# Copies that move a product to the other 64 partitions, made by VectorE instead of ScalarE in two of the six passes

## The chip, the cores and the metric

The kernel runs on one core of one Trainium2 chip. The metric is the time of the whole program on the device in microseconds (us), median over its runs; lower is better. TensorE multiplies matrices from SBUF into PSUM, which here is eight banks of 128 partitions by 512 float32 values. VectorE, ScalarE and GpSimd work on tiles beside it.

## The reference, cut to what matters

The program computes two model blocks of two layers each, for 256 positions of width 1024, in float32. The part that the change touches is in layer 0 of the first block: a recurrence over 256 context and 256 latent positions, run forwards and backwards.

```python
def _rwkv7_scan(S0, r, w, k, v, kk, a):
    def step(S, inp):
        r_t, w_t, k_t, v_t, kk_t, a_t = inp
        sa = jnp.einsum('bhvk,bhk->bhv', S, kk_t)
        S = (S * w_t[:, :, None, :] - sa[..., None] * (kk_t * a_t)[:, :, None, :]
             + v_t[..., None] * k_t[:, :, None, :])
        return S, jnp.einsum('bhvk,bhk->bhv', S, r_t)
...
    yf_c, Sf_c = _rwkv7_scan(S0, r_c, wf_c, k_c, v_c, kk_c, a_c)
    yf_l, _ = _rwkv7_scan(Sf_c, r_l, wf_l, k_l, v_l, kk_l, a_l)
```

There are 8 heads of 64 channels. Everything else of the two blocks (attention, other recurrences, projections, gated layers) is left as it is.

## The kernel before, in words

The recurrence is computed in 8 chunks of 64 positions. `rwkv_chunks_stage(net, d)` does it once for each direction: d = 0 forwards, and later in the program d = 1 backwards. Two heads share a tile, one in the lower and one in the upper 64 partitions (`o` is the half, `half(o)` its slice), and two chunks make a pair, `cp`; the four pairs are handled in the order x = 0 to 3, with PSUM banks 2x and 2x+1 for pair x. Within a chunk the positions depend on each other, so each head needs the inverse of a 64 by 64 triangular matrix. The kernel builds it in `N_LEVELS` = 5 levels, each of which doubles the size of the blocks inverted so far.

A stage is a block of its own with a barrier at its end; all its engines run their own instruction streams and wait for each other by semaphores. In the streams of one chunk stage stand:

- TensorE: `products` of the keys for each pair (L3172, L3182, L3183) and transposes (L3189); then `across` (L3199) for x = 0 to 3, the products with values, called level 0 below; then a hardware loop of five passes (L3215, `pe.Fori`), each with four `across` for the level and, behind them, four inverse products (L3231, L3232). The loop's register arithmetic sets the values waited for. Every `across` fills half a bank for chunk q = 0 and half a bank for q = 1; the inverse product needs both copied to SBUF, that of q = 1 with its halves of partitions exchanged.
- ScalarE: `copy_tokens` (L2848), the copies of the transposes, 32 in a stage; then per level (0 to 5) and pair one copy of 128 partitions for q = 0 (L3322) and two of 64 partitions that exchange the halves for q = 1 (L3324). The last of the three raises `y_copied`.
- VectorE: masks on the products (L3344, L3349); then per level and pair two subtractions that update the inverse (L3358), and in the first seven cases one multiplication by the decays (L3362). They raise `doubled`.
- GpSimd: masks for the next level (L3304, L3298), raising `level_ready`.

After the fifth level the chunks are gone through one by one (L3240 to L3287 on TensorE, L3367 to L3391 on VectorE). SyncE issues no transfers in this stage. The trace shows small transfers of 16 KB on queue 8, which the profile calls instruction.

## Time and profile before

| what | value |
|---|---|
| median of 3 runs | 2006.39 us (2005.78 to 2009.97) |
| the profiled execution, its own time | 2003.86 us |
| its span, first to last instruction | 2002.0 us |
| granted TensorE clock, mean over the span | 0.966 of full speed |
| TensorE busy with matmuls | 1849.9 us (92%) |
| VectorE busy | 1252.0 us (63%) |
| ScalarE busy | 858.9 us (43%) |

A row of the profile that groups instructions names line, engine, operation and tiles, the count, busy time and mean of one in ns. A row of the timeline gives start and length in us, and in brackets how long the engine stood idle before and what released it. "issue" there means that the profile shows nothing that the engine waited for. Times in the trace count from the span's start. The clock of TensorE is given as a share of its full 2.4 GHz, so 0.50 is 1.2 GHz.

### The profile page before, as it was taken

Reading aid. Unit: us, or ns where it says so; the run is one execution under the profiler, and the core shown is the slowest. Engines: PE = TensorE matmul, PEld = TensorE weight load, DVE = VectorE, ACT = ScalarE, POOL = GpSimd, SP = SyncE. Lnnn points to the kernel's source line nnn. Section 1 sums busy time; section 2 is a strip of 40 time slices with the busy share of each in tenths; the row PEclk is TensorE's granted clock in tenths of the full one; section 3 lists DMA queues with packets and bytes.
Section 4 is the critical chain, followed back from the end, with each engine's and each line's share of the span. In section 5 each row is a group of like instructions: output and inputs, shape, how many; then the busy total and the mean of one; then the engine's idle time right before and its main releaser. Section 6 shows DMA issues by size and latency. Waiting matters only on the chain. (4 is left out here: it accounts for less than half of the span.)

```text
span 2002.0 us, 42924 instructions
## 1 busy us (share of the span) xinstructions
PE 1849.9 (92%) x18352; PEld 1619.1 (81%) x18352; DVE 1252.0 (63%) x2170; ACT 858.9 (43%) x1588; POOL 289.3 (14%) x341
## 2 busy tenths in 40 slices
PE   7999887878899999999999699999789999889997
PEld 5787546857588888888878699999589999679997
DVE  4574786676657523543766778745668756677753
ACT  4321566446334211221537445534654345564432
POOL 0201203314040000013002111012030012021001
PEclk8999888979999999999999899999899999999998
DMA  9752750020523232322420356554135465225543
GB/s 323 208 175 84 255 188 3 2 65 2 163 76 100 85 105 84 105 85 85 147 64 1 100 178 188 188 185 155 43 127 190 148 190 190 85 85 190 190 153 100
DMA packets 248982, 254.68 MB, mean 127 GB/s; under 512 B 6914, under 2 KB 247186, under 8 KB 248690
## 3 DMA queue, kind: packets, MB, share of 16 engines
q1 hardware_dynamic: 239214, 242.85, 37.9%
q10 hardware_dynamic: 8740, 8.51, 1.3%
q8 instruction: 121, 1.98, 0.4%
q0 software_dynamic: 864, 0.98, 0.3%
q14 instruction: 43, 0.35, 0.1%
HBM read 251.28 MB, written 1.05 MB: 126 GB/s over the span
## 5 line engine op out<-in xcount | busy, mean ns | idle before, releaser
L529 DVE TENSOR_TENSOR RING_rounded<-RING,SC_rounded 128x1024 fp32r<-128x1024 f32 (+2 forms) x390 | 462.1, 1227 | 229.9 <-ACT SC_rounded L522 229.4
L549 PE MATMUL bank<-OT_rounded,SC_rounded 128*128 128x256 f32 (+1 forms) x1808 | 575.7, 318 | 14.5 <-DVE HT_rounded L1115 6.8
L550 PE MATMUL bank<-HT_rounded,SC_rounded 128*128 128x256 f32 (+1 forms) x1808 | 570.8, 316 | 0.0
L551 PE MATMUL bank<-OT_rounded,RING_rounded 128*128 128x256 f32 (+1 forms) x1808 | 569.2, 315 | 0.0
L522 ACT ACTIVATE SC_rounded<-RING 128x1024 fp32r<-128x1024 f32 (+2 forms) x390 | 372.6, 1006 | 331.2 <-DMA RING<-in_l_mlp_w 184.1
L549 PEld LDWEIGHTS bank<-OT_rounded,SC_rounded 128*128 128x128 f32 x1808 | 343.5, 190 | 43.8 <-DVE HT_rounded L1115 7.6
L551 PEld LDWEIGHTS bank<-OT_rounded,RING_rounded 128*128 128x128 f32 x1808 | 342.8, 190 | 25.5
L550 PEld LDWEIGHTS bank<-HT_rounded,SC_rounded 128*128 128x128 f32 x1808 | 342.9, 190 | 21.7
L549 PE MATMUL bank<-PT_rounded,SC_rounded 128*128 128x256 f32 (+1 forms) x896 | 277.6, 310 | 5.1 <-DVE RING_rounded L529 5.1
L550 PE MATMUL bank<-PT_rounded,SC_rounded 128*128 128x256 f32 (+1 forms) x896 | 276.7, 309 | 0.0
L551 PE MATMUL bank<-PT_rounded,RING_rounded 128*128 128x256 f32 (+1 forms) x896 | 276.0, 308 | 0.0
L549 PEld LDWEIGHTS bank<-PT_rounded,SC_rounded 128*128 128x128 f32 x896 | 168.5, 188 | 17.0 <-DVE RING_rounded L529 6.3
L551 PEld LDWEIGHTS bank<-PT_rounded,RING_rounded 128*128 128x128 f32 x896 | 168.3, 188 | 10.7
L550 PEld LDWEIGHTS bank<-PT_rounded,SC_rounded 128*128 128x128 f32 x896 | 168.4, 188 | 9.5
L550 PE MATMUL bank<-OT_rounded,SC_rounded 128*128 128x256 f32 (+1 forms) x336 | 101.2, 301 | 0.0
L549 PE MATMUL bank<-HT_rounded,SC_rounded 128*128 128x256 f32 (+1 forms) x272 | 84.3, 310 | 13.4 <-DVE OT_rounded L1468 5.5
L796 DVE SCALAR_TENSOR_TENSOR XT<-bank,MOD,XT 128x256 f32<-128x256 f32 x48 | 21.3, 479 | 112.6 <-PE bank L551 112.6
L551 PE MATMUL bank<-HT_rounded,RING_rounded 128*128 128x256 f32 (+1 forms) x272 | 83.1, 306 | 0.0
L3358 DVE TENSOR_TENSOR SC<-SC,bank 128x512 f32<-128x512 f32 (+1 forms) x80 | 50.9, 681 | 35.6 <-PE bank L3232 35.1
L776 ACT ACTIVATE PT<-bank 128x512 f32<-128x512 f32 x32 | 18.9, 598 | 123.6 <-PE bank L551 123.6
L838 DVE TENSOR_TENSOR PT<-PT 128x512 f32<-128x512 f32 x32 | 22.1, 690 | 74.7 <-ACT PT L776 74.7
L550 PEld LDWEIGHTS bank<-OT_rounded,SC_rounded 128*128 128x128 f32 x336 | 64.8, 193 | 2.2
(570 smaller groups left out, 2805.9 us busy)
## 6 DMA issues: line engine op xcount, KB each, us to landing
RING<-in_l_mlp_w SPq DMA_DIRECT2D x64, 1024.0 KB, 5.3
RING<-in_w_ffn_in SPq DMA_DIRECT2D x44, 1024.0 KB, 5.1
RING<-in_l_mod_w SPq DMA_DIRECT2D x32, 1024.0 KB, 5.5
RING<-in_l_w_in SPq DMA_DIRECT2D x25, 1024.0 KB, 6.3
RING<-in_w_ffn_out SPq DMA_DIRECT2D x16, 768.0 KB, 4.8
RING<-in_w_in SPq DMA_DIRECT2D x10, 1024.0 KB, 5.2
RING<-in_w_ffn_out SPq DMA_DIRECT2D x16, 640.0 KB, 4.3
PT<-in_l_mod_w SPq DMA_DIRECT2D x8, 1024.0 KB, 10.4
```

The costliest lines, as they stand in the source:

```text
L522: act.activation(net.high4(s, m)[:, 0:self.w.kts[s], :], net.ring_half(net.RING, s, m, self.w.kts[s]), ACT.Copy).then_inc(self.high_ready, 1)
L529: net.nc.vector.tensor_tensor(low, whole, net.high4(s, m)[:, 0:self.w.kts[s], :].bitcast(F32), ALU.subtract).then_inc(self.split_ready, 1)
L549: net.nc.tensor.matmul(bank[:, tokens], high, x_high, start=start, stop=False)
L550: net.nc.tensor.matmul(bank[:, tokens], high, x_low, start=False, stop=False)
L551: return net.nc.tensor.matmul(bank[:, tokens], low, x_high, start=False, stop=stop)
L776: act.activation(hidden.whole[:, 2 * q + m, :], part.bank(q, m)[:, :], ACT.Relu).then_inc(part.taken, 1)
L796: return nc.vector.scalar_tensor_tensor(into, bank[:, tokens], net.MOD[:, gate + tile, j:j + 1], into, ALU.mult, ALU.add)
L838: link(nc.vector.tensor_tensor(whole, whole, whole, ALU.mult))
L3358: nc.vector.tensor_tensor(inv, inv, bank, ALU.subtract).then_inc(doubled, 1)
```

## The change

At level 0 and at level 1 the two copies that exchange the halves go from ScalarE to VectorE. ScalarE keeps the plain copy and raises `y_copied` after it. VectorE raises a new semaphore, `y_swapped`, for which TensorE waits too, once in every `across` and once in every inverse product of the loop. From level 2 on ScalarE makes all three copies as before.

```diff
             with pe.Fori(0, N_LEVELS):
                 for x, cp in enumerate(pairs):
                     pe.wait_ge(y_copied, y_done(0, x))
+                    pe.wait_ge(y_swapped, y_done(0, x))
                     pe.wait_ge(level_ready, level_at)
...
                 for x, cp in enumerate(pairs):
+                    pe.wait_ge(y_swapped, y_done(1, x))
                     pe.wait_ge(y_copied, y_at)
...
-                    act.activation(first, same, ACT.Copy)
-                    for h in range(2):
+                    step = act.activation(first, same, ACT.Copy)
+                    for h in range(2 if lv > 1 else 0):
                         step = act.activation(second[half(1 - h)], swapped[half(h)], ACT.Copy)
                     step.then_inc(y_copied, 1)
...
+            for lv in range(2):
+                for x, cp in enumerate(pairs):
+                    dve.wait_ge(y_ready, y_done(lv, x))
+                    swapped = net.ps[2 * x + 1][:, 0:256].rearrange("p (t m) -> p t m", t=4)
+                    second = mem.y[x][1] if lv else mem.gram[:, 2 * cp + 1, 1, :, 0, :]
+                    for h in range(2):
+                        step = nc.vector.tensor_copy(second[half(1 - h)], swapped[half(h)])
+                    step.then_inc(y_swapped, 1)
             for lv in LV:
```

On ScalarE, where level 0 and level 1 of the forward stage stand, the program before has these rows (RING is the tile of level 0, PT and SC those of `mem.y`):

```order
L2848 ACTIVATE HT<-bank 64x4x64 x4
L3322 ACTIVATE RING<-bank 128x4x64
L3324 ACTIVATE RING<-bank 64x4x64 x2
...
L3322 ACTIVATE PT<-bank 128x256
L3324 ACTIVATE PT<-bank 64x256 x2
...
L3322 ACTIVATE SC<-bank 128x256
L3324 ACTIVATE SC<-bank 64x256 x2
```

The changed program has these at the same place, with its own line numbers (L3324 is now the plain copy, L3326 the exchange):

```order
L2848 ACTIVATE HT<-bank 64x4x64 x4
L3324 ACTIVATE RING<-bank 128x4x64 x4
L3324 ACTIVATE PT<-bank 128x256 x2
L3324 ACTIVATE SC<-bank 128x256 x2
L3324 ACTIVATE PT<-bank 128x256
L3326 ACTIVATE PT<-bank 64x256 x2
```

The first eight plain copies now follow each other, and the exchanges begin at level 2. On VectorE the sixteen exchanges stand between the last mask and the first subtraction (L3368, which was L3358):

```order
L3351 TENSOR_TENSOR SC<-bank,CONST 128x256 x4
L3359 COPY RING<-bank 64x4x64 x8
L3359 COPY PT<-bank 64x256 x4
L3359 COPY SC<-bank 64x256 x4
L3368 TENSOR_TENSOR SC<-SC,bank 128x2x256 x2
L3372 TENSOR_TENSOR PT<-PT,SC 128x4x128
```

In the difference of TensorE's rows, with what each waits for, the first `across` of the loop reads so:

```order
-L3219 REGISTER_ALU [waits rwkv_chunks0_level_ready,rwkv_chunks0_y_copied]
-L3221 REGISTER_ALU [waits rwkv_chunks0_doubled]
+L3220 REGISTER_ALU [waits rwkv_chunks0_level_ready,rwkv_chunks0_y_swapped,rwkv_chunks0_y_copied]
+L3222 REGISTER_ALU [waits rwkv_chunks0_doubled]
 L3199 MATMUL bank<-SC 64x64 x16
```

No matmul moves; one wait is added ahead of each of the 8 groups of matmuls of a pass, 40 in a stage of five passes.

## Rows read from the trace of the kernel before

**Rows 1.** The page, parts 1 and 3; windows over both stages up to level 5
```profile
PE 1849.9 (92%) x18352; PEld 1619.1 (81%) x18352; DVE 1252.0 (63%) x2170; ACT 858.9 (43%) x1588; POOL 289.3 (14%) x341
...
q8 instruction: 121, 1.98, 0.4%
...
core 0: us, PE busy (x) PEld busy (x) DVE busy (x) ACT busy (x) POOL busy (x), PEclk, DMA share, GB/s
317.00:380.00 63.00, 52.37 (x2584) 49.05 (x2578) 43.50 (x77) 39.52 (x104) 33.27 (x44) 0.96 0.01 2
437.00:495.50 58.50, 52.14 (x2507) 48.40 (x2500) 40.30 (x73) 39.53 (x104) 33.66 (x44) 0.94 0.01 3
```

**Rows 2.** Timeline of ScalarE, forward stage, levels 0 and 1
```profile
333.51 1.55 ACT L2848 ACTIVATE HT<-bank 64x256 f32<-64x256 f32 x4
335.08 0.39 ACT L3322 ACTIVATE RING<-bank 128x256 f32<-128x256 f32 x1
335.48 0.77 ACT L3324 ACTIVATE RING<-bank 64x256 f32<-64x256 f32 x2
336.27 0.38 ACT L3322 ACTIVATE RING<-bank 128x256 f32<-128x256 f32 x1
...
343.81 0.77 ACT L3324 ACTIVATE SC<-bank 64x256 f32<-64x256 f32 x2
```

**Rows 3.** Timeline of VectorE, forward stage
```profile
331.97 1.40 DVE L3349 TENSOR_TENSOR SC<-bank,CONST 128x256 f32<-128x256 f32 x4
342.35 1.28 DVE L3358 TENSOR_TENSOR SC<-SC,bank 128x512 f32<-128x512 f32 x2 [8.98 <-PE bank L3232]
343.55 0.68 DVE L3362 TENSOR_TENSOR PT<-PT,SC 128x512 f32<-128x512 f32 x1
...
348.64 1.28 DVE L3358 TENSOR_TENSOR SC<-SC,bank 128x512 f32<-128x512 f32 x2
```

**Rows 4.** Timeline of TensorE, forward stage: level 0's last group and pass 1
```profile
335.20 0.69 PE L3199 MATMUL bank<-SC,RING 64*64 64x64 f32 x32 [0.99 <-ACT HT L2848]
336.47 0.69 PE L3199 MATMUL bank<-SC 64*64 64x64 f32 x32 [0.58 <-ACT RING L3324]
...
340.04 0.69 PE L3199 MATMUL bank<-SC 64*64 64x64 f32 x32 [0.50 <-ACT RING L3324]
341.13 0.24 PE L3231 MATMUL bank<-PT,SC 64*64 64x64 f32 x1 [0.40 <-ACT PT L3324]
...
344.54 0.27 PE L3231 MATMUL bank<-PT,SC 64*64 64x64 f32 x1 [1.16 <-issue]
...
348.23 0.27 PE L3231 MATMUL bank<-SC 64*64 64x64 f32 x1 [1.60 <-issue]
348.94 3.65 PE L3199 MATMUL bank<-SC 64*64 64x64 f32 x128 [0.36 <-issue]
```

**Rows 5.** Windows of the forward stage: instruction transfers and TensorE's stops
```profile
337.00:338.00 1.00, 0.51 (x33) 0.41 (x28) 0.00 (x0) 0.95 (x4) 0.73 (x2) 1.00 0.08 16
342.00:343.00 1.00, 0.97 (x66) 0.86 (x60) 0.65 (x2) 0.95 (x3) 0.00 (x0) 1.00 0.05 16
345.00:346.00 1.00, 1.00 (x83) 1.00 (x78) 1.00 (x2) 0.00 (x0) 0.00 (x0) 1.00 0.07 16
347.00:348.00 1.00, 0.00 (x0) 0.00 (x0) 1.00 (x3) 0.00 (x0) 0.00 (x0) 1.00 0.00 0
344.50:348.00 3.50, 2.09 (x127) 1.96 (x127) 3.06 (x6) 0.07 (x1) 0.00 (x0) 1.00 0.02 5
348.00:353.00 5.00, 4.41 (x179) 4.30 (x183) 2.50 (x5) 2.79 (x8) 4.08 (x7) 0.66 0.00 0
```

**Rows 6.** Timeline of TensorE, backward stage: level 0's end and pass 1
```profile
452.19 0.57 PE L3199 MATMUL bank<-SC,RING 64*64 64x64 f32 x21 [0.17 <-issue]
454.56 0.97 PE L3199 MATMUL bank<-SC 64*64 64x64 f32 x32 [0.58 <-ACT RING L3324]
455.75 3.51 PE L3199 MATMUL bank<-SC 64*64 64x64 f32 x96 [0.21 <-ACT RING L3324]
461.45 0.26 PE L3231 MATMUL bank<-PT,SC 64*64 64x64 f32 x1 [0.18 <-issue]
465.47 0.21 PE L3231 MATMUL bank<-SC 64*64 64x64 f32 x1 [1.86 <-issue]
466.86 0.35 PE L3199 MATMUL bank<-SC 64*64 64x64 f32 x9 [0.23 <-issue]
```

**Rows 7.** Durations by source line: VectorE's copy, ScalarE's exchange
```profile
L3377 DVE COPY SC<-bank x2: 409/409/409, 381.9 to 497.7; 128x256 f32<-128x256 f32 x2
L3324 ACT ACTIVATE SC<-bank x40: 376/380/382, 342.6 to 493.7; 64x256 f32<-64x256 f32 x40
L3358 DVE TENSOR_TENSOR SC<-SC,bank x80: 673/679/692, 342.4 to 497.1; 128x512 f32<-128x512 f32 x64, 64x512 f32<-64x512 f32 x16
```

**Rows 8.** Timelines of ScalarE and TensorE, a later pass
```profile
366.62 0.38 ACT L3322 ACTIVATE PT<-bank 128x256 f32<-128x256 f32 x1 [3.51 <-PE bank L3199]
...
370.58 0.77 ACT L3324 ACTIVATE SC<-bank 64x256 f32<-64x256 f32 x2
373.61 0.38 ACT L3322 ACTIVATE PT<-bank 128x256 f32<-128x256 f32 x1 [2.26 <-PE bank L3199]
...
372.86 2.44 PE L3199 MATMUL bank<-SC 64*64 64x64 f32 x128 [0.22 <-DVE SC L3358]
```

More of the change, by code:

```diff
@@ L3158, in rwkv_chunks_stage @@
         kv_ready, values_ready, values_copied = st.sem("kv_ready"), st.sem("values_ready"), st.sem("values_copied")
-        own, decayed = st.sem("dve_own"), st.sem("decayed")
+        own, decayed, y_swapped = st.sem("dve_own"), st.sem("decayed"), st.sem("y_swapped")
         carried = lambda j: (mem.far if j % 2 else mem.near)[:, :, chunks[j] // 2]
```

## The prediction

> **What bounds the kernel now.** I read the page first, then windows over the two chunk stages, then one engine's timeline after the other. The page's shares say little here: TensorE is busy 92% of the program [rows 1], but this change lives in levels 0 and 1 of two stages, 63.0 and 58.5 us long with all that leads up to them [rows 1], of 2002.0. The stages are closed by barriers and issue no transfers of weights, so what one of them gains should reach the end nearly whole.
>
> In the forward stage ScalarE ends the copies of the transposes at 335.06 and goes straight on with 8 groups of copies, 0.39 + 0.77 and a short gap, one group every 1.19 us, until 344.58 [rows 2]. VectorE ends its masks at 333.37 and then stands idle for 8.98 us [rows 3]. TensorE starts its last group of level 0 at 335.20 and then waits 0.58 to 0.40 us before each of five groups, released by ScalarE's exchange each time [rows 4]. Read that far, ScalarE is the bound and VectorE is free.
>
> The reader should read one row further. At 344.54 TensorE comes back from an idle 1.16 us, and at 348.23 from 1.60 us, both put down to "issue" [rows 4]. The second stands in the middle of the inverse product of pair 3, whose copy was done at 344.58: nothing that the change touches holds it. The page has a queue named instruction, with 121 transfers of 1.98 MB in all, 16 KB each [rows 1]. The windows show 16 KB moved in the microsecond from 342, and 16 KB in that from 345, and TensorE at rest from 347 to 348 [rows 5]. Between the two stops 127 matmul and 127 weight-load rows lie [rows 5], with the register instruction ahead of each product (one or two here) about 256 instructions: a block of code, which TensorE consumes and then stands still until the next has come. The backward stage repeats it, with stops that end at 452.19, 461.45 and 465.47 [rows 6]. From the second pass on the same code is run again and such stops don't recur.
>
> The crossings into a new block, counted back by 256 instructions, lie in the forward stage at about 335.9 (the loop's start), 340.5 (near the end of the fourth `across`), 344.54 and 348.23; in the backward one at 452.19, 457.1 (early in the third `across`), 461.45 and 465.47 [rows 4, 6]. So a block comes 3.7 to 4.4 us after the one before it was entered, and usually about 4.0. Only two crossings, 340.5 and 457.1, are late because of ScalarE: TensorE arrived there after the code.
>
> **The change, part by part.** *Removed from ScalarE:* 2 exchanges by 4 pairs by 2 levels by 2 stages, 32 by 0.38 [rows 7] = 12.2 us. Level 0 gets a pace of 0.40 us a pair in place of 1.19.
>
> *Added on VectorE:* the same 32 copies. No row shows a PSUM copy of 64 partitions by 256; the nearest is one of 128 by 256 at 409 ns [rows 7]. The lower bound is nothing, the upper the 679 ns of an operation on 512 columns [rows 7]. I take 0.41, the same columns and source, so at most 0.82 a pair and 6.6 a stage. The cover is the idle 8.98 us. At 0.82 a pair level 0's exchanges start at 333.4 and the fourth, whose product ends near 335.9, is done by 336.8; TensorE can't enter the next block before 339.6, so even at 1.36 a pair (done at 338.8) it stays hidden. Without that cover the two of the last pair would cost 0.8 a level. Queued behind them is VectorE's first subtraction, which starts at 342.35 now [rows 3]; level 1's last exchange should end by about 341, so it is not late.
>
> The Trainium skill ("VectorE: DVE Perf Modes", the errata section's cycle table) prices a PSUM copy at 120 + columns cycles of 0.96 GHz on VectorE and 172 + columns of 1.2 GHz on ScalarE; I estimate from it 392 ns against 357, so it speaks against the move by 0.035 each, or 1.1 us if all 32 lay on the path. The rows here say 409 against 380, the same sign; as they lie in parallel with ScalarE and with the wait for code, neither puts anything into the sum.
>
> *Gain, forward stage.* Data no longer delays TensorE: its fourth `across` of the loop would reach the crossing at 335.9 + 4 by 0.59 (a group of 32 takes 0.69, overlapping the next by 0.1 [rows 4]) = 338.3. The code comes at 335.9 + 4.0 = 339.9 (339.6 with 3.7) instead of a crossing at 340.5. The next two follow by the same intervals: 343.7 and 347.5 instead of 344.54 and 348.23. I take 0.9 (0.6 by intervals of 4.0, 1.2 by 3.7).
>
> *Gain, backward stage.* 452.19 + 4.0 = 456.2, and TensorE's data is there by 455.3; then 460.2 and 464.2 instead of 465.47, a gain of 1.3. If the load isn't asked for earlier than now it is 0.7. I take 1.0.
>
> *Added on TensorE:* 40 waits a stage. I take each as one more instruction of the sequencer, which no row of the trace shows by itself. Where the loop turns, the idle is 0.36 and 0.23 us [rows 4, 6] for the branch, register work and three waits, so one is at most 0.12 and may be nothing where the sequencer runs ahead; I take 0.1. In pass 1 the wait for code hides all. In passes 2 to 5 ScalarE copies without a pause from 366.62 to 371.35 at 1.19 a pair [rows 8], slower than TensorE's inverse product (66 matmul rows in 0.97 us [rows 5], so 64 in 0.95), so the waits ahead of inverse products 2 to 4 lie under its copies. Exposed is the one ahead of the first `across` of a pass, which comes right behind the branch: 4 passes by 2 stages by 0.1 = 0.8 us.
>
> *Sum:* -0.9 - 1.0 + 0.8 = -1.1 us. The profiled execution took 2003.86 (span 2002.0), so it would take about 2002.8; the median of the runs shown lies 2.5 above the profiled one, and 2006.4 - 1.1 = 2005.3.
>
> **The rivals.**
>
> *Code is not the limit.* If the blocks came as early as TensorE wanted them, the forward loop would turn at 335.9 + 4 by 0.59 + 4 by 0.95 = 342.1 in place of 348.9. VectorE then limits: its first subtraction starts at 335.9 + 4 by 0.59 + 0.95 = 339.3, and at 1.28 + 0.68 less an overlap of 0.1 a pair its fourth ends at 339.3 + 3 by 1.86 + 1.28 = 346.2, now 349.92 [rows 3]. That is 3.7 us earlier, and the `across` behind it at full clock gives up to 1.2 more: some 4 to 5 us a stage, 9 together, less 0.8 for the waits: 1998. For it speaks ScalarE's release of five groups [rows 4]; against it two stops with nothing else to wait for and a 16 KB transfer ahead of each [rows 5]. By the Trainium skill ("Runtime: NRT & Kernel Launch", Instruction fetch mechanics) the sequencer fetches the next 16 KiB block, 256 instructions, while the present one runs, and crossing is mostly hidden: by that rule this rival would come true. The trace agrees on the size of a block and not on the hiding: 1.16, 1.60 and 1.86 us of stop. 8 in 100.
>
> *The gain is eaten.* The load is asked for no earlier, the stages gain 0.3 and 0.5, and the waits take 0.8 or a little more, as more of them show: 2006 to 2008. 16 in 100.
>
> *The waits decide, slower.* TensorE's own pace is the limit in passes 2 to 5 and all 80 waits show: 80 by 0.1 = 8, less 1.9, is +6, so 2012.5. It counts as slower from about 60 of 80 exposed. Against it is ScalarE's slower pace there [rows 8]. 5 in 100.
>
> *The clock moves.* After the two stops of the forward stage the granted clock is 0.66 from 348 to 353, that is partly 1.2 GHz, and four `across` take 3.65 us [rows 5, 4] where they take 2.44 at full clock [rows 8]: 1.2 us. In the backward stage level 1's three groups take 3.51 for 96 matmuls [rows 6]. Which stretch runs at the lower level may change, as TensorE rests earlier and longer before a load; one such stretch more or less is 1 to 2 us either way, and up to 4 if it hits both stages: 11 in 100, of which 4 end faster than 0.2%, 2 slower (the forecast already lies on the fast side) and 5 between.
>
> **How the numbers follow.** 0.2% of 2006.4 is 4.0 us, about what a measurement of this kernel can tell from none. The forecast as summed has the other 60 in 100. Faster by more than that: the first rival's 8, and 4 for clock and block boundaries falling well. Slower: the wait rival's 5, and 2 of the clock's. The rest, 81, is the same. The range leaves out the first and third rival at their full size, and takes in the bounds of the loads, the clock and the 2.5 us between executions: 2001.0 to 2008.5.
>
> **What the profile after would show.** Right: ScalarE's plain copies 0.40 apart at levels 0 and 1 and 64-partition COPY rows of about 0.41 on VectorE in its former idle time; TensorE's waits for ScalarE at 336.47 to 341.13 gone, and in their place longer "issue" stops, ending some 4 us apart, with the 16 KB transfers ahead of them; the loop's first turn only 0.5 to 1.3 us earlier after the last transposes than now; later passes at 7.0 us (373.61 - 366.62 [rows 8]) as before or 0.1 longer. Wrong: a first turn near 342 would make the first rival true; a pass of 7.4 or more the third; exchanges over 0.7 us, or a VectorE that ends them after 342.3, would break the cover. Since code shifts by 8 instructions in the loop, a stop can also fall just before the end of a product on which VectorE waits; the sum has nothing for that.

## The result, and the profile after

The changed kernel took 2008.43 us (median of 20 runs, 2002.98 to 2013.80), the kernel before 2005.40 in its 20 runs beside it (2002.29 to 2009.97). The ratio is 1.0016, 95% interval [1.0009, 1.0024]: slower by a little, within 0.2%. The forecast was right that the change is small, and had the sign wrong: 1.1 us faster was summed, 3.0 us slower was measured.

The page, and the two stages in windows, to be read against [rows 1]:

```profile
PE 1858.6 (93%) x18352; PEld 1625.7 (81%) x18352; DVE 1267.1 (63%) x2202; ACT 846.4 (42%) x1556; POOL 287.4 (14%) x341
...
q8 instruction: 121, 1.98, 0.4%
...
core 0: us, PE busy (x) PEld busy (x) DVE busy (x) ACT busy (x) POOL busy (x), PEclk, DMA share, GB/s
317.00:380.00 63.00, 54.10 (x2587) 50.63 (x2579) 50.97 (x93) 33.38 (x89) 33.45 (x44) 0.94 0.01 2
437.00:495.50 58.50, 50.48 (x2333) 47.11 (x2329) 45.62 (x85) 31.57 (x84) 33.30 (x44) 0.91 0.01 3
```

ScalarE gave 32 exchanges (858.9 to 846.4 us, x1588 to x1556), VectorE took them. Fewer matmuls lie in the backward window than before (2333, before 2507): the stage is late there. ScalarE and VectorE in the forward stage, against [rows 2, 3]:

```profile
335.10 1.26 ACT L3324 ACTIVATE RING<-bank 128x256 f32<-128x256 f32 x4
337.49 0.85 ACT L3324 ACTIVATE PT<-bank 128x256 f32<-128x256 f32 x2 [1.14 <-PE bank L3199]
...
333.41 3.52 DVE L3359 COPY RING<-bank 64x256 f32<-64x256 f32 x8
337.49 1.74 DVE L3359 COPY PT<-bank 64x256 f32<-64x256 f32 x4 [0.56 <-PE bank L3199]
...
341.21 0.86 DVE L3359 COPY SC<-bank 64x256 f32<-64x256 f32 x2 [1.09 <-PE bank L3199]
342.26 1.29 DVE L3368 TENSOR_TENSOR SC<-SC,bank 128x512 f32<-128x512 f32 x2 [0.18 <-PE bank L3234]
```

Eight exchanges take 3.52 us, 0.44 each (0.41 was taken), and they end before VectorE's first subtraction, which starts at 342.26 as it did (342.35). TensorE's first pass, against [rows 4] and, for the backward stage, [rows 6]:

```profile
335.22 0.69 PE L3199 MATMUL bank<-SC,RING 64*64 64x64 f32 x32 [0.99 <-ACT HT L2848]
336.74 2.13 PE L3199 MATMUL bank<-SC 64*64 64x64 f32 x122 [0.83 <-POOL SC L3300]
340.82 0.34 PE L3199 MATMUL bank<-SC 64*64 64x64 f32 x6 [1.95 <-issue]
...
344.72 0.37 PE L3233 MATMUL bank<-PT,SC 64*64 64x64 f32 x1 [1.03 <-issue]
348.72 0.35 PE L3234 MATMUL bank<-SC 64*64 64x64 f32 x1 [0.29 <-issue]
```

```profile
456.72 1.15 PE L3199 MATMUL bank<-SC 64*64 64x64 f32 x61 [1.21 <-issue]
460.71 0.21 PE L3234 MATMUL bank<-SC,PT 64*64 64x64 f32 x1 [1.90 <-issue]
464.89 0.26 PE L3233 MATMUL bank<-SC 64*64 64x64 f32 x1 [0.76 <-issue]
```

The waits for ScalarE at 336.47 to 341.13 are gone: 122 matmuls run through. In their place stand stops that end at 336.74, 340.82, 344.72 and 348.72, that is 4.1, 3.9 and 4.0 us apart, the last three for nothing that the profile shows. (The first row names GpSimd, but its product for this pair was done at 324.8.) A 16 KB transfer on the instruction queue starts ahead of each of the last three, at 338.14, 342.05 and 345.95. The intervals of about 4.0 us are as forecast; only the chain started 0.8 us late (336.74, where 335.9 was assumed), so all of it is later than the forecast 339.9, 343.7 and 347.5, and no earlier than before. Such a late start needs no change of the kernel: TensorE's sequencer rests 0.79 us ahead of the loop here, 0.09 in the profile of before, and 0.68 in a second profile of the same kernel before. The granted clock is 0.50 from 343 to 348, where before had full clock up to 348; the stops become shorter by it and end no later. In the backward stage the stops end at 456.72, 460.71 and 464.89, the last two 0.7 and 0.6 us earlier than before (forecast 460.2 and 464.2).

One later pass is seen best in ScalarE, whose first copy of a pass follows TensorE's first group at a fixed distance:

```profile
366.03 0.38 ACT L3324 ACTIVATE PT<-bank 128x256 f32<-128x256 f32 x1 [3.55 <-PE bank L3199]
373.17 0.38 ACT L3324 ACTIVATE PT<-bank 128x256 f32<-128x256 f32 x1 [2.40 <-PE bank L3199]
```

7.14 us, where [rows 8] have 6.99 (373.61 - 366.62).

**How the experiments are compared.** Every kernel was run some 12 times (the one with a filler 6), with 23 to 35 runs of the kernel before beside it; single runs of one kernel spread over 3 to 13 us. Much of that spread follows the mean granted clock of the run: over 383 runs (two with a clock of 0.918 and 0.919, one of before and one of the code shift, are left out, as the line doesn't fit them) a straight line with one constant for each kernel has a slope of -0.93 +- 0.04 us for 0.001 of clock, and leaves 1.5 us. So beside each ratio stands the kernel's constant minus that of before, "at the same clock", with its standard error; an unchanged copy shows what that is worth. For the changed kernel it is +1.3 +- 0.4 (against the runs of before in the other sets, as the clocks of the 20 beside it are not on record). What a change costs by lowering the clock itself is not in that column; the section behind the experiments comes to it.

### The profile page after: what moved, and what is told of

It is laid out like the page before. It is cut to its first block and busy times, and to the rows that moved or that the text cites. A ratio compares the mean times of both kernels' runs of the same rounds, so it can differ in the third digit from the quotient of the medians.

```text
span 2006.4 us, 42966 instructions
## 1 busy us (share of the span) xinstructions
PE 1858.6 (93%) x18352; PEld 1625.7 (81%) x18352; DVE 1267.1 (63%) x2202; ACT 846.4 (42%) x1556; POOL 287.4 (14%) x341
## 5 line engine op out<-in xcount | busy, mean ns | idle before, releaser
L550 PEld LDWEIGHTS bank<-HT_rounded,SC_rounded 128*128 128x128 f32 x1808 | 342.9, 190 | 21.8
L549 PEld LDWEIGHTS bank<-HT_rounded,SC_rounded 128*128 128x128 f32 x272 | 52.8, 194 | 16.7 <-DVE RING_rounded L529 9.9
```

Of the source, the lines that this page charges most:

```text
L549: net.nc.tensor.matmul(bank[:, tokens], high, x_high, start=start, stop=False)
L550: net.nc.tensor.matmul(bank[:, tokens], high, x_low, start=False, stop=False)
```

## The experiments

**The kernel before again**, not a character changed.

> The kernel before, run as if it were a new one: the floor of the comparison, and the granted clock beside the time of each of its runs. Two theories stand for the 3.2 us (0.16%) that the change costs. Clock theory: the change by itself costs nothing, but TensorE's rests lie earlier and longer, the granted clock falls to 1.2 GHz in stretches that are on the path, and the time of a run follows its mean granted clock; the kernel before then has a higher mean clock, by about 0.002 or more, than the changed one's runs (0.960 to 0.969, mean about 0.963), and the two lie on one line of time over clock. Wait theory: the 80 added waits on TensorE cost it directly; the clocks are then the same, and at the same clock the changed kernel is 3 us slower. Both expect 1.000 here, within 0.001.

2003.62 against 2006.15, ratio 0.9993 [0.9982, 1.0003], at the same clock +0.1 +- 0.5. Its mean clock was 0.0014 above that of the others: a difference of 1.2 us in the mean comes by chance, and the column at the same clock removes it.

**The waits alone.** TensorE's stream is that of the changed kernel, ScalarE makes all copies and raises the new semaphore after its plain copy.

```diff
-                    act.activation(first, same, ACT.Copy)
+                    step = act.activation(first, same, ACT.Copy)
+                    if lv < 2:
+                        step.then_inc(y_swapped, 1)
```

> The 40 added waits a stage alone: ScalarE makes all copies as in the kernel before, and raises y_swapped itself, earlier than y_copied, so that no wait holds anything longer. Wait theory: all or most of the loss, +2 to +3.5 us (1.0010 to 1.0017). Clock theory: only the wait at the loop's turn shows, +0.8 us (1.0004), and the granted clock is that of the kernel before. In the profile a later pass of the forward stage should take 7.0 us plus 0.1 by either.

2009.37, ratio 1.0016 [1.0004, 1.0028], at the same clock +1.5 +- 0.5: the waits without any copy moved cost as much as the whole change.

**The copies alone.** The exchanges move to VectorE, but ScalarE waits for them; TensorE's stream is that of before.

```diff
+                    if lv < 2:
+                        act.wait_ge(y_swapped, y_done(lv, x))
-                    act.activation(first, same, ACT.Copy)
-                    for h in range(2):
+                    step = act.activation(first, same, ACT.Copy)
+                    for h in range(2 if lv > 1 else 0):
```

> The whole move of copies to VectorE, with TensorE's stream left exactly as in the kernel before: no added wait there. ScalarE waits for y_swapped ahead of its plain copy at levels 0 and 1 and then raises y_copied for both. Wait theory (the added waits cost some 1.2 us directly and lower the granted clock by about 0.002, worth 2 us more): the loss is gone, ratio 0.999 to 1.0000, mean clock 0.965 or more, and later passes take 7.0 us. If the moved copies themselves lower the clock by making TensorE's rests in pass 1 longer: mean clock about 0.963 and ratio 1.001.

2004.70, ratio 0.9988 [0.9977, 1.0000], at the same clock -1.8 +- 0.5. What the move itself gives is near the summed -1.9; the step that failed lies in the waits.

**Data sooner.** The changed kernel with the copies of levels 0 and 1 cut short, and `mem.y` zeroed at the stage's start. The edit does less than its expectation says: its rows are 64x64 and 128x64, so 64 of 256 columns are copied and not 4, in 0.22 us in place of 0.42 on VectorE and 0.38 on ScalarE. It leaves out the other 192 columns.

> The changed kernel with the copies of levels 0 and 1 cut to one column of each head's 64 (the rest of those products is left out and stands as zeros written at the stage's start), so the data of pass 1 is there almost at once. If the blocks of code set the pace of pass 1, the loop of the forward stage turns where it does in the changed kernel (349.1, 14.0 us after the last group of level 0 at 335.2) or at most 0.5 us earlier, and the time stays within 2 us of the changed kernel's. If the copies set it, the loop turns near 342 to 343 and the time falls by 8 us or more (0.997 against the kernel before).

2007.98, ratio 1.0007 [0.9994, 1.0020], at the same clock +1.1 +- 0.5. Copies a quarter of the size gain nothing clear of the error over the changed kernel (+1.3), and the first pass still stops, until 338.85, 342.75 and 346.66, 3.9 us apart. The first rival ("Code is not the limit") is out.

**One wait for four.** The changed kernel with one wait for four pairs ahead of the loop, and one a pass ahead of the inverse products.

```diff
+            pe.wait_ge(y_swapped, 4)
             with pe.Fori(0, N_LEVELS):
...
-                    pe.wait_ge(y_swapped, y_done(0, x))
...
+                pe.wait_ge(y_swapped, 8)
...
-                    pe.wait_ge(y_swapped, y_done(1, x))
```

> The change with its copies on VectorE, but with one wait ahead of the loop and one a pass ahead of the inverse products in place of eight a pass. Wait theory: the loss goes away and the gain of 1 to 1.9 us that the summing gave is seen (0.9990 to 0.9996). Clock theory: still slower by 2 to 3 us (1.0010 to 1.0015), as the rests of pass 1 are as long as in the changed kernel, or longer since inverse product 0 waits for the exchange of pair 3.

2007.58, ratio 1.0004 [0.9992, 1.0017], at the same clock +1.3 +- 0.5. A later pass takes 7.00 to 7.03 again, and the time is not back: the number of waits isn't all of it. One wait for four also holds the first pass until the last pair's exchange is done, so this run doesn't isolate the number.

**A shift of the code, no wait.** The kernel before with two unused 64x64 matmuls a stage ahead of the loop, which put all that follows 8 instructions further.

```diff
+                if x == 0:
+                    for n in range(2):
+                        nc.tensor.matmul(net.ps[0][half(0), 256 + at(n).start:256 + at(n).stop], ident[half(0), half(0)],
+                                         ident[half(0), half(0)], start=True, stop=True)
```

> The kernel before with two matmuls of 64 by 64 more ahead of level 0 in each stage (8 instructions on TensorE, no further wait, the result unused), so that all code behind them lies 8 and then 16 instructions later, as the change does it. If the place of the code blocks makes the loss: 1.001 or more. If it doesn't: 1.0000, mean clock 0.965, with some 0.1 us for the matmuls.

2008.37, ratio 1.0014 [1.0001, 1.0028], but its clock was low: at the same clock +0.6 +- 0.5. The same two matmuls in the variant with the copies alone:

> The variant in which ScalarE waits for VectorE's copies (-1.8 us at the same clock), plus the two unused 64x64 matmuls a stage ahead of the products with values that shift all that follows by 8 instructions. Theory A: no wait added, so the gain stays but for the 0.1 us that the matmuls take: -1.5 +- 0.5 us at the same clock, ratio 0.9992. Rival (the place of the rows in the 16 KB blocks of code takes the first pass's gain away): 0 to +0.5 us at the same clock, ratio 1.0000 to 1.0005, and the first pass of a stage no shorter than before.

2006.56, ratio 1.0004 [0.9995, 1.0012], at the same clock +0.3 +- 0.5, 2.1 +- 0.6 above the variant without them. The rival written there fits: 8 more instructions in front can cost. Beside before they cost +0.6 +- 0.5, so their size is less sure, and that they act by their place in the blocks of code is not shown by these two runs.

**A filler.** The changed kernel with one unused 128x256 matmul a pass ahead of the fourth `across`.

> The changed kernel with one matmul of 128 by 256 more in each pass of the loop, ahead of the fourth group with values, into a free half of a bank (its result unused). It takes some 0.4 us of TensorE's time in each pass, under ScalarE's copies. If the loss comes by way of the granted clock because TensorE rests a little too much in the passes: the mean clock goes up to 0.965 or more and the time goes down by 1 us or more against the changed kernel (1.001 or less against the one before). If the waits cost directly alone: clock as in the changed kernel (0.963) and 1 to 3 us slower than it (1.002 to 1.003).

2013.09, ratio 1.0039 [1.0025, 1.0054], at the same clock +6.5 +- 0.6. Ten such matmuls cost 5 us over the changed kernel, and no clock is bought with them. TensorE's idle time there isn't free.

**The last pair.** The kernel before with the exchange of pair 3 on VectorE at all levels, ScalarE waiting for it.

> From the kernel before: VectorE makes the two exchanges of the last pair (x = 3) at every level, 0 to 5, and ScalarE waits for them ahead of its plain copy of that pair; TensorE's stream is unchanged. Where ScalarE sets the pace of a pass (7.0 us: four groups of 1.19 and the turn), its last group shrinks by 0.77 us, VectorE being idle 1.84 us just then. If passes 4 and 5 and partly 2 and 3 are bound by ScalarE: passes 4 and 5 take about 6.4 us and the time falls by 2 to 4 us (0.998 to 0.999). If TensorE's own time in a pass (about 6.3 us with the turn) or VectorE binds right behind: under 1 us.

2004.25, ratio 0.9993 [0.9982, 1.0004], at the same clock -1.1 +- 0.5; a pass at full clock takes 6.73. Together with the copies alone (levels 0 and 1 of all pairs, levels 2 to 4 of pair 3):

> VectorE makes the exchange of all four pairs at levels 0 and 1 and that of pair 3 at levels 2 to 4; ScalarE waits for it ahead of its plain copy, and TensorE's instructions are those of the kernel before. The two parts alone gave -1.7 and -1.0 us at the same clock (the second with level 5, where it lengthened the chunk phase by 0.6 a stage). Theory that what the copies give is real and additive: -2.5 to -3 us, ratio 0.9985 to 0.9988, passes at full clock 6.73 to 6.75 us from pass 2 on and the fill pass shorter by 1 us a stage. Rival (code blocks limit the first pass, so only one of the two shows there; and a shorter pass lowers or shifts the clock): -1.5 to -2, ratio 0.9991.

2005.17, ratio 0.9996 [0.9984, 1.0008], at the same clock -0.4 +- 0.5: the two gains don't add up. The theory missed; the passes did come to 6.73 and 6.78, and the third pass took 8.46 in the backward stage (7.71 in the copies alone). In that kernel VectorE's last multiplication by the decays takes 1.12 us, where the copies alone have 0.68; the section on VectorE and GpSimd below shows what that comes from.

**Which waits.** The waits alone, cut to those ahead of `across`, and to those ahead of the inverse products.

> ScalarE keeps all copies; of the 80 added TensorE waits only the 40 ahead of the products with values stay (20 a stage). Every one of them but those of level 0 stands ahead of an `across` group. Theory A (each added wait costs its time wherever it stands, the number decides): half of what all 80 cost against the kernel before at the same granted clock (1.5 us), so +0.8, and half of the fall of the mean clock (0.0019), so -0.001; in all about +1.7 us, ratio 1.0008. Theory B (only waits that stand in front of a group that starts when a product is just done cost, which my prediction had: the first group of `across` of a pass): +0.8 of time here and nothing from the waits ahead of the inverses; a pass at full clock 7.10 us. Theory C (the rows' place in the code blocks decides, not the waits): a change of 1 to 3 us in the length of passes 2 and 3 against the kernel before, in either direction, with the time in no order with the number of waits.

> The other half: only the 40 added TensorE waits ahead of the inverse products (20 a stage). Theory A: +0.8 us at the same clock, clock lower by 0.001, in all +1.7 us, ratio 1.0008, as for the waits ahead of `across`. Theory B: nothing, time as before within 0.5 us at the same clock, a pass at full clock 7.00 us. Theory C: 1 to 3 us in passes 2 and 3, in either direction.

2006.13, 1.0003 [0.9992, 1.0013], at the same clock -0.3 +- 0.5; and 2008.69, 1.0013 [1.0003, 1.0024], +1.7 +- 0.5. ScalarE's first copies of two passes, first kernel, then second:

```profile
366.54 0.38 ACT L3323 ACTIVATE PT<-bank 128x256 f32<-128x256 f32 x1 [3.52 <-PE bank L3199]
373.53 0.38 ACT L3323 ACTIVATE PT<-bank 128x256 f32<-128x256 f32 x1 [2.26 <-PE bank L3199]
```

```profile
367.58 0.38 ACT L3323 ACTIVATE PT<-bank 128x256 f32<-128x256 f32 x1 [3.55 <-PE bank L3199]
374.72 0.39 ACT L3323 ACTIVATE PT<-bank 128x256 f32<-128x256 f32 x1 [2.40 <-PE bank L3199]
```

6.99 and 7.14 us. It is the other way round than forecast: the waits ahead of the inverse products are paid, those ahead of `across` are not. Theories A and B both missed.

**Twice the waits.** A second satisfied wait behind each of the 80.

> All 80 added TensorE waits and, behind each, one more on a second semaphore that has long been raised: 160 added waits. Theory A: twice what 80 cost: +3.0 us at the same clock, clock lower by 0.004, in all +6.6 us, ratio 1.0033; a pass at full clock 7.25 us. Theory B: +0.8 becomes +1.6, clock no lower than with 80, in all about +4, 1.002. Theory C: no order with the number; between 0.999 and 1.002, and a pass at full clock still 7.13.

2008.79, 1.0012 [1.0003, 1.0021], at the same clock +2.8 +- 0.5, pass 7.20. The lower clock that was expected did not come.

**The order of the waits.** In the changed kernel and in the waits alone, the order ahead of `across` turned round; and in the waits ahead of `across` alone, the added wait moved to the last place.

```diff
+                    pe.wait_ge(y_swapped, y_done(0, x))
                     pe.wait_ge(y_copied, y_done(0, x))
-                    pe.wait_ge(y_swapped, y_done(0, x))
                     pe.wait_ge(level_ready, level_at)
```

The expectations of the first two have this wrong: ahead of the inverse products the changed kernel and the waits alone already wrote the added wait in front of the one for ScalarE's copies, as the diff of the change shows, and the edit left it there. So their theory A was not put to the test at the place where the cost lies.

> The changed kernel, with one thing turned round: each of the 80 added TensorE waits stands ahead of the wait for ScalarE's copies and no longer behind it. Number of instructions, copies and semaphores are as in the changed kernel. Theory A (a wait costs only where it stands behind the wait that ends last: ahead of the inverse products that is the wait for ScalarE's copies, so that the added one is worked off after the data is there, 0.12 us in a pass): all of the cost of the waits goes, a pass at full clock takes 7.00 us and not 7.13, pair 3's inverse products start 5.61 us into a pass and not 5.76, and the time is that of the variant in which ScalarE waits: -1.8 us against the kernel before at the same clock, ratio 0.9991. Theory B (each wait costs by being there, or the shift of the code that the added instructions make costs): as the changed kernel, +1.3 us at the same clock, ratio 1.0010 to 1.0016, pass 7.13. A mix (pass 7.00 but time still above -1): the order of the waits is the smaller part, and something else in the first pass is the rest.

> ScalarE keeps all copies; the 80 added waits are there, each ahead of the wait for ScalarE's copies. Theory A: the added waits cost nothing: 0 +- 0.5 us against the kernel before at the same clock (behind it: +1.5), ratio 1.0000, pass at full clock 7.00 us. Theory B: +1.5 us, ratio 1.0010 to 1.0016.

> ScalarE keeps all copies; only the 40 added waits ahead of the products with values, but each as the last of the waits there, behind the one for the inverse (`doubled`), where the variant before had it second of four and cost nothing. Theory A (behind the wait that ends last, it is paid): up to 0.1 us at the first group of each pass, and at pair 3's group, 0.1 to 0.2 us a pass, pass at full clock 7.10 to 7.20, +1 to +2 us at the same clock. Theory B (its place among the waits does not matter, waits ahead of `across` are cheap): 0 +- 0.5 us, pass 7.00.

2007.48, 1.0009 [0.9998, 1.0019], +1.3 +- 0.5; 2009.39, 1.0015 [1.0005, 1.0024], +2.5 +- 0.5; 2009.50, 1.0015 [1.0005, 1.0025], +1.7 +- 0.5. The first two kept their passes of 7.10 to 7.18. The third made passes of 7.10 to 7.14 out of 6.99 with the same number of waits. TensorE's own records of its sequencer, beside the matmuls, say why: they show which instruction carries which wait. (A semaphore has a number there; that of y_copied is known from before, whose inverse products wait for nothing else.) Microseconds from the first weight load of a pass at full clock, around pair 3's inverse products:

```
                semaphore instruction   register addition    first weight load
before          none                    y_copied   5.552     5.612
waits_values    none                    y_copied   5.553     5.613
changed         y_copied   5.555        y_swapped  5.696     5.756
wait_ahead      y_copied   5.544        y_swapped  5.684     5.745
```

A register addition carries one wait. A second one makes a semaphore instruction of its own in front of it. Which wait goes where follows the source in every kernel here: the one written first goes to the addition, the rest to the semaphore instruction (ahead of `across` it is y_copied that the addition carries in the changed kernel, and y_swapped with the order turned round). Ahead of the inverse products the added wait was written first. So the addition got y_swapped, long raised, and the semaphore instruction got y_copied, the wait that ends last; the addition is then worked off only behind it. That costs 0.11 to 0.14 us. With y_copied written first, the semaphore instruction would hold the satisfied wait and could be worked off ahead of time. No run tried that.

The Trainium skill ("Perfetto Trace Analysis", Identifying Dependency Chains) says that EventSemaphore instructions may be inserted ahead of an instruction that waits for several engines; the trace agrees and adds the price. Ahead of `across` before already had such an instruction with one wait in it, and the added one went into it free. Written last, behind the first addition, it made another one there (at 6.977, for 0.1 us at a pass's start).

**A register addition to carry it.** The changed kernel with an addition on an unread register behind the wait.

> The changed kernel with the same number of TensorE instructions and waits, one thing arranged otherwise: ahead of the inverse products the wait for VectorE's copies is carried by a register addition of its own (on a register that nothing reads), so that no separate semaphore instruction (two waits in one) is made there. In the traces with a second wait there, such an instruction stood 0.14 us ahead of the register addition and that 0.06 us ahead of the first weight load, with the group of pair 3 at 5.76 us into a pass and a pass of 7.13 us; without it the addition follows the copy directly, 5.61 and 7.00. Theory A (what costs is the semaphore instruction that stands between the wait that ends last and the group): pair 3's group at 5.61 to 5.65, pass at full clock 7.00 to 7.04, and the time 1.3 us under the changed kernel's at the same clock, about 0 against the kernel before, or -1.8 if that is all that keeps it from the variant in which ScalarE waits. Theory B (any added instruction costs its 0.1 us there, whichever it is and wherever it waits): 7.10 to 7.13, +1.3 at the same clock. Theory C (the shift of the code): pass 7.00 and the time still +1.2 at the same clock, ratio 1.0006 or above.

2005.58, 1.0003 [0.9991, 1.0015], +0.8 +- 0.5. The edit did not do what it says: the addition was dropped in compiling, and the trace has the semaphore instruction at 5.549 and a pass of 7.10, like the changed kernel. So it is one more sample of the changed kernel's stream, and tells nothing of theory A. With the changed kernel and the one with the waits in the other order there are 44 runs of that stream, with a mean 2.1 us above the kernel before.

**One semaphore instruction less.** The copies alone, and ahead of `across` the wait for ScalarE's copies behind the additions.

```diff
-                    pe.wait_ge(y_copied, y_done(0, x))
                     pe.wait_ge(level_ready, level_at)
                     pe.reg_add(level_at, level_at, 1)
                     pe.wait_ge(doubled, inverse_at)
                     pe.reg_add(inverse_at, inverse_at, 2)
+                    pe.wait_ge(y_copied, y_done(0, x))
```

> The variant in which ScalarE waits for VectorE's copies (-1.9 us at the same clock), and in the products with values the wait for ScalarE's copies of level 0 moved behind the two register additions, where it is carried by the first multiplication. Before, it shared a semaphore instruction with the wait for the levels, and that instruction stood at a pass's start 0.106 us ahead of the first register addition, 0.26 us ahead of the first weight load, on the path that sets the pass. Theory A: that instruction goes from all 20 groups a stage, and at the first group of each pass its 0.10 us comes off: pass at full clock 6.90 instead of 7.00, five passes a stage in two stages make -1.0, with the copies' gain -2.9 us at the same clock, ratio 0.9986. Rival (ScalarE sets the pass, so an earlier start only moves the wait to pair 3): pass 7.00, -1.9; or the 4 instructions that each pass is shorter by put the first pass's stops for code elsewhere: +-1 us in the first pass alone.

2002.74 against 2005.52, ratio 0.9991 [0.9980, 1.0002], at the same clock -2.3 +- 0.5.

```profile
464.46 0.38 ACT L3324 ACTIVATE PT<-bank 128x256 f32<-128x256 f32 x1 [6.54 <-PE bank L3199]
...
471.35 0.38 ACT L3324 ACTIVATE PT<-bank 128x256 f32<-128x256 f32 x1 [2.15 <-PE bank L3199]
```

A pass of 6.89, as theory A had it. Its time is the lowest of the study, but only 0.5 +- 0.6 us under the copies alone at the same clock, where 1.0 was expected: that the shorter pass reaches the end is not shown.

## Where the rest went: a block's end, the clock, VectorE and GpSimd

The semaphore instruction explains 0.12 us in each of 4 passes (the first hides it) of 2 stages, 1.0 us. A fit over 294 runs of the twelve kernels that differ only in three things gives: copies moved -1.0 +- 0.3, semaphore instruction ahead of the inverse products +2.1 +- 0.3, 8 instructions of shift +1.1 +- 0.4. About 1.1 is left beside the visible 1.0, and a shift of the code alone costs the same.

This fit holds the clock fixed, and so hides what the waits do to the clock. A fit of the same form to the mean clocks themselves gives -0.0015 +- 0.0003 for the semaphore instruction, -0.0011 +- 0.0005 for the shift and +0.0005 +- 0.0004 for the copies. To the times without the clock it gives +3.5 +- 0.4, +2.1 +- 0.6 and -1.4 +- 0.4 us. So some 1.4 us more go with the waits by way of a lower clock. In which part of the program the clock falls isn't shown.

The traces show where the stages differ. In the backward stage's pass 1, TensorE's last stop comes after this many of the pass's 256 weight loads of inverse products; 192 of them belong to pairs 0 to 2. The counts are of recorded loads, and some 10 of 256 are missing from each profile:

```
                     loads before stop   VectorE starts pair 2, before pass 2   passes 2 + 3
before                      193                 1.96 us                            14.75 us
before again                193                 2.05                               16.92
copies alone                193                 2.04                               14.75
waits ahead of across       193                 1.77                               15.24
changed                     190                 1.51                               17.64
waits alone                 190                 1.22                               16.91
waits, other order          190                 1.22                               18.05
code shift                  185                 1.07                               16.92
copies alone + shift        185                 1.08                               17.90
```

With 193 the stop lies about at the end of pair 2's product. A few instructions more in front, and the last loads of pair 2 fall behind the stop, so VectorE gets that product up to 1 us later. But the two rows of the kernel before have the same instructions and the same place of the stop, and 2.2 us between them in passes 2 and 3. What differs between them is the granted clock: from 464.5 to 469.5 it is 1.00 in the first and 0.66 in the second, and in the forward stage it is the other way round, with 16.94 us for passes 2 and 3 in the first and 15.62 in the second.

So it is in all twenty profiles. TensorE has a stretch at 1.2 GHz in passes 2 and 3 in 24 of the 40 stages, and those take 16.4 to 18.0 us; the other 16 have at most 0.15 us of it and take 14.8 to 15.8, but for the kernel with the filler (16.5 and 17.6). The six kernels whose TensorE stream before the stop is that of before have the stretch in 1 backward and 5 forward stages, the thirteen with more instructions there in 12 backward and 4 forward ones. So the shift goes with a stretch at the lower clock in the backward stage in place of the forward one; what moves it is not shown.

VectorE in the copies alone, backward stage:

```profile
465.13 1.28 DVE L3368 TENSOR_TENSOR SC<-SC,bank 128x512 f32<-128x512 f32 x2
466.33 0.69 DVE L3372 TENSOR_TENSOR PT<-PT,SC 128x512 f32<-128x512 f32 x1
...
469.76 0.70 DVE L3372 TENSOR_TENSOR PT<-PT,SC 128x512 f32<-128x512 f32 x1
...
471.58 0.68 DVE L3372 TENSOR_TENSOR PT<-PT,SC 128x512 f32<-128x512 f32 x1
...
473.38 0.68 DVE L3372 TENSOR_TENSOR PT<-PT,SC 128x512 f32<-128x512 f32 x1
```

The same in the changed kernel, with GpSimd's level products below:

```profile
468.40 1.17 DVE L3372 TENSOR_TENSOR PT<-PT,SC 128x512 f32<-128x512 f32 x1
...
471.97 1.04 DVE L3372 TENSOR_TENSOR PT<-PT,SC 128x512 f32<-128x512 f32 x1
...
474.13 0.68 DVE L3372 TENSOR_TENSOR PT<-PT,SC 128x512 f32<-128x512 f32 x1
...
475.93 1.12 DVE L3372 TENSOR_TENSOR PT<-PT,SC 128x512 f32<-128x512 f32 x1
...
467.20 5.27 POOL L3300 TENSOR_TENSOR SC<-RING,CONST 128x256 f32<-128x256 f32 x8 [8.44 <-PE bank L3234]
474.37 5.56 POOL L3300 TENSOR_TENSOR SC<-RING,CONST 128x256 f32<-128x256 f32 x8 [1.90 <-PE bank L3234]
```

The multiplication by the decay (L3372), which has both operands and its result in SBUF, takes 0.68 us. Of the 280 such rows in twenty profiles 103 take over 0.8 us, and each of these overlaps one of GpSimd's level products (0.64 us alone) by 0.29 us or more; where none overlaps, the row takes 0.68. In the copies alone the three of pass 2 start as a GpSimd product ends, or in its pause, and keep 0.68 to 0.70, and it is GpSimd's next row that grows to 1.10 or 1.18. Who comes first keeps its time, and the other waits. The Trainium skill ("SBUF — State Buffer", "SBUF: two separate sides") has this as a rule: VectorE with two inputs in SBUF and GpSimd take a shared pair of ports for a whole instruction, and the later one is blocked. The trace agrees: no row of the two is longer than both together, 0.68 + 0.64. TensorE in pass 3, the copies alone and then the changed kernel:

```profile
472.34 1.94 PE L3199 MATMUL bank<-SC 64*64 64x64 f32 x96 [0.26 <-issue]
475.38 0.69 PE L3199 MATMUL bank<-SC 64*64 64x64 f32 x32 [1.10 <-DVE SC L3368]
```

```profile
474.53 1.16 PE L3199 MATMUL bank<-SC 64*64 64x64 f32 x64 [0.26 <-DVE SC L3368]
476.14 0.69 PE L3199 MATMUL bank<-SC 64*64 64x64 f32 x32 [0.45 <-DVE SC L3368]
478.38 0.97 PE L3199 MATMUL bank<-SC 64*64 64x64 f32 x32 [1.54 <-DVE SC L3368]
...
478.00:483.00 5.00, 4.62 (x209) 4.66 (x213) 1.96 (x4) 1.94 (x6) 1.93 (x4) 0.66 0.00 0
```

1.10 us of wait for VectorE became 0.45 and 1.54, and behind it the granted clock is 0.66 over 478 to 483: 1.2 GHz in part, right after that wait. Pass 3 took 10.06 us, 7.71 in the copies alone. Over all profiles passes 2 and 3 of the backward stage took 14.8 to 16.9 us (mean 15.4) in the six kernels named above, and 16.4 to 18.1 (mean 17.6) in the thirteen. In the forward stage the thirteen were quicker, 16.2 against 16.7, so 1.7 of the 2.3 us are left over both stages; 0.4 to 0.5 of that are semaphore instructions. Each profile is a single execution, so how much of it a mean over runs holds is less sure than its place. Which part the clock has and which the meeting of VectorE and GpSimd stays open: the meeting is read from their rows and was not tried by itself, by taking the decay away, say.

## Why the prediction was wrong, point by point

- *Code blocks bound the first pass*: right. The stops come about 4 us apart in the changed kernel and with the short copies, and cutting the copies gained nothing. The Trainium skill's "mostly hidden" ("Runtime: NRT & Kernel Launch", Instruction fetch mechanics) does not hold here: 1.95 and 1.03 us of stop in the rows above.
- *VectorE's copies, 0.41 each, hidden*: right, 0.42 to 0.43 a row and 0.44 at its pace; level 0's take 3.52 us in the idle time.
- *Gain -0.9 and -1.0*: alone -1.8 +- 0.5, as summed. Over all pairs of kernels with and without the move it is -1.0 +- 0.3, so the term was too large by up to half. In the changed kernel's own profile the forward blocks were no earlier, and the backward ones 0.6 to 0.7 us earlier where 1.0 was taken.
- *Added waits, +0.8, exposed only ahead of the first `across` of a pass*: **this step failed.** The text put the waits ahead of the inverse products "under its copies", since ScalarE is slower there than TensorE. But ScalarE's slower pace is why TensorE waits there, and what is worked off after the awaited copy lies on the path: at pair 3 it makes the pass 0.11 to 0.14 us longer. The wait ahead of `across` was free, as it shared an instruction. At the same clock the fit has +2.1 +- 0.3 instead of +0.8: 1.0 for the instruction itself, and 1.1 whose cause is not isolated. With the fall of the clock it is +3.5 +- 0.4, and the sum had nothing for that fall.
- *"A stop can also fall just before the end of a product on which VectorE waits; the sum has nothing for that"*: it happened, in the backward stage, and is a likely owner of part of that 1.1; the stretch at 1.2 GHz, which sits in passes 2 and 3 there in 12 of 13 such kernels, is another.
- Sum by the fit: -1.0 + 2.1 = +1.1, measured +1.3 +- 0.4 at the same clock. The changed kernel's 20 runs also had a mean clock 0.0019 lower, the other 1.7 us. The same stream in the other two kernels was 0.0008 lower and 0.0003 higher, so part of that may be chance, but not all: over the six kernels with the semaphore instruction the clock is lower by the 0.0015 +- 0.0003 above. Without the clock the fit sums to -1.4 + 3.5 = +2.1.
- *Rivals*: "Code is not the limit" is refuted. "The waits decide" had the right place, the inverse products, and the wrong size: one group in four is paid, and it came to 2 us, not 8. "The gain is eaten" is what happened, just above its 2006 to 2008, and by another way. "The clock moves" had more in it than its 11 in 100: the stretch at 1.2 GHz changes place between profiles (1.3 and 2.2 us in the two stages of the two profiles of before), and the mean clock falls with the added waits; whether it is cause or consequence of the longer waits in pass 3 is open. That the time came out above before, and within the range stated, is no credit to the sum: its term for the waits was too small by 1.3 to 2.7 us.

## What to carry to other kernels

A satisfied wait isn't free where it makes the engine's instruction stream one longer behind the wait that ends last: count instructions between the awaited event and the first useful one, look in the trace which of them carries which wait, and let the producer that already signals do the extra waiting (-1.8 +- 0.5 us here, where the change as made has +1.3 +- 0.4). Where code stops for its blocks, as here every 4 us in a first pass, ask which product's end lies near a stop. Where two engines share the work of a loop, look at the rows whose duration has two values, and ask what a move does to which of them meet. Before a difference between two profiles is put down to a change, take a second profile of the kernel before: here it differed from the first by 2.2 us in two passes.

## What was unexpected of the hardware

- Of two waits in front of a register addition, one gets a semaphore instruction of its own, in every kernel here the one written second. It costs TensorE 0.11 to 0.14 us where it is the wait that ends last.
- A VectorE multiplication with all operands in SBUF, 128x512, takes 0.68 us, and up to 1.22 where GpSimd's product was first; GpSimd's go from 0.64 to as much as 1.18 where VectorE was.
- Single runs follow the mean granted clock at 0.93 us for each 0.001, so of two kernels with the same instructions one had a mean 1.2 us lower over 12 runs.
